# A hybrid decoder layer on one core: the second half's dense units are placed anew among the expert steps, a part of gelu is moved six steps later, and softplus is computed in another form

## What is computed

```
xn = rmsnorm(h); q,k,v,cx,cb,cc,ga,gc = split(xn @ w_in)
# 1. stick-breaking attention (16 heads of 64, causal), beside a gated short convolution of 3 taps
z = q @ k.T / 8
log_stay  = where(s < t, log_sigmoid(-z), 0)          # = -softplus(z)
log_after = reverse_cumsum(log_stay) - log_stay
w = where(s < t, exp(log_sigmoid(z) + log_after), 0);  y_attn = w @ v
y_conv = cb * conv3(cc * cx)
h += (sigmoid(ga) * (y_attn @ w_a) + sigmoid(gc) * (y_conv @ w_c)) @ w_out
# 2. cross attention over 256 memory tokens, 4 heads
h += softmax(rmsnorm(h) @ wq @ memk.T / 16) @ memv @ wo
# 3. expert mixer: 8 heads; two top-16 searches over 128 keys, then the best 16 of the 256 pairs
u = expert_u[idx]; act = gelu(u . rmsnorm(h)); h += sum(gate * act * expert_v[idx])   # 128 experts a token
out = rmsnorm(h)
```

## Time and profile before

| | us |
|---|---|
| median of 3 runs | 2285.18 |
| lowest, highest | 2284.89, 2292.32 |
| the profiled execution | 2279.03 |
| its span in the trace | 2276.9 |
| TensorE busy | 2034.0 (89%) |
| VectorE busy | 1223.6 (54%) |
| ScalarE busy | 397.9 (17%) |

### The profile page before, as it was taken

The page is one execution under the profiler, slowest core; times in us unless marked ns, Lnnn a source line. Parts: engine busy times, 40 slices in busy tenths (PEclk is TensorE's granted clock), DMA queues, the critical chain, the costliest instruction groups (busy, mean ns, idle before and its releaser), DMA issues.

```text
span 2276.9 us, 24064 instructions
## 1 busy us (share of the span) xinstructions
PE 2034.0 (89%) x9031; PEld 1305.2 (57%) x9031; DVE 1223.6 (54%) x3078; ACT 397.9 (17%) x947; POOL 904.8 (40%) x785
## 2 busy tenths in 40 slices
PE   8999999989798889998889278899999878999997
PEld 7577886746685777785748245533333445333332
DVE  0132100013975888785748999943343999553201
ACT  2222210111212233211111022200000222100001
POOL 0000000000762333553426677754444888664422
PEclk9999999999899999999899578799999788899999
DMA  7322344324997776898859888999999999999976
GB/s 236 124 93 84 126 159 149 113 90 137 384 365 251 240 238 231 314 382 295 303 203 327 310 311 309 333 372 342 342 340 344 329 336 332 332 402 375 364 254 202
DMA packets 252440, 613.48 MB, mean 269 GB/s; under 512 B 18677, under 2 KB 121125, under 8 KB 252325
## 3 DMA queue, kind: packets, MB, share of 16 engines
q0 software_dynamic: 110592, 402.70, 49.5%
q1 hardware_dynamic: 141120, 208.17, 26.5%
q10 hardware_dynamic: 612, 1.07, 0.1%
HBM read 609.77 MB, written 2.10 MB: 269 GB/s over the span
## 4 chain that ended last, share of the span: by engine, by line
PE 72%; DVE 19%; DMA 3%; ACT 2%; issue 2%; POOL 1%; DVEq 0%; POOLq 0%; SPq 0%; ACTq 0%
PE ps L514 28%; PE ps L725 20%; PE ps L526 9%; DVE u_rows L1189 7%; PE ps L688 7%; DVE hot_a L1245 2%; PE ps L551 2%; PE ps L715 2%; PE ps L563 1%; DVE hot_b L1253 1%; DVE hot_b L1248 1%; PE ps L537 1%; DMA wring<-in_peer_w_query_dram 1%; DMA v_rows<-in_peer_v_dram,idx_turned 1%; PE ps L660 1%
## 5 line engine op out<-in xcount | busy, mean ns | idle before, releaser
L476 POOL DMA_INDIRECT u_rows<-in_peer_u_dram,idx x512 | 613.6, 1198 | 1048.5 <-DVE idx L1176 562.7
L1189 DVE CUSTOM_DVE_ANT_0 u_rows<-u_rows,xn 128x1024 f32<-128x1024 f32 x512 | 618.3, 1216 | 212.3 <-DMA u_rows<-in_peer_u_dram,idx 210.5
L514 PE MATMUL ps<-xT,wring 128*128 128x256 f32 x2560 | 578.5, 386 | 10.7 <-DVE xT L977 4.9
L514 PEld LDWEIGHTS ps<-xT,wring 128*128 128x128 f32 x2560 | 492.7, 194 | 80.7 <-DVE xT L977 4.9
L725 PE MATMUL ps<-d_rows,gates 128*128 128x512 f32 x1024 | 457.1, 599 | 0.0
L725 PEld LDWEIGHTS ps<-d_rows,gates 128*128 128x128 f32 x1024 | 189.1, 190 | 268.3 <-issue 268.3
L688 PE MATMUL ps<-v_rows,diag 64*64 64x512 f32 x2048 | 290.1, 689 | 25.2 <-DMA v_rows<-in_peer_v_dram,idx_turned 25.0
L488 POOL DMA_INDIRECT v_rows<-in_peer_v_dram,idx x128 | 146.5, 1145 | 267.0 <-PE ps L688 244.5
L715 PEld LDWEIGHTS ps<-hot_b,hot_a 128*128 128x128 f32 x1024 | 151.7, 235 | 136.1 <-DVE hot_b L1253 116.7
L715 PE MATMUL ps<-hot_b,hot_a 128*128 128x64 f32 x1024 | 161.5, 324 | 75.3 <-DVE hot_b L1253 75.2
L908 ACT ACTIVATE diag<-ident,wgt 128x64 f32<-128x64 f32 x256 | 75.8, 335 | 577.3 <-PE ps L688 526.5
(11 more groups left out here) (167 smaller groups left out, 1799.9 us busy)
## 6 DMA issues: line engine op xcount, KB each, us to landing
wring<-in_w_in_dram SPq DMA_DIRECT2D x128, 512.0 KB, 5.9
d_rows<-in_peer_v_dram SPq DMA_DIRECT2D x128, 512.0 KB, 6.8
wring<-in_peer_w_query_dram SPq DMA_DIRECT2D x32, 512.0 KB, 6.6
wring<-in_w_branch_conv_dram SPq DMA_DIRECT2D x16, 512.0 KB, 6.1
wring<-in_w_branch_attn_dram SPq DMA_DIRECT2D x16, 512.0 KB, 4.6
wring<-in_w_out_dram SPq DMA_DIRECT2D x16, 512.0 KB, 4.9
wring<-in_xattn_wq_dram SPq DMA_DIRECT2D x16, 512.0 KB, 4.7
wring<-in_xattn_wo_dram SPq DMA_DIRECT2D x16, 512.0 KB, 5.6
```

What stands on the lines that cost most here:

```text
L476: pool.indirect_dma_start(out=u_rows[:, n % URING, :], out_offset=None, in_=peer_u[0], in_offset=bass.IndirectOffsetOnAxis(ap=idx[:, g % I ...
L514: mm = pe.matmul(bank(job)[:, 0:HN], w[:, k % 4, P * b:P * (b + 1)], act[:, k, :], start=(k == 0), stop=(k == KT - 1))
L1189: dve.tensor_tensor_reduce(out=u, in0=u, in1=(xn2 if h else xn1)[:, i, :], scale=1.0, scalar=0.0, op0=ALU.mult, op1=ALU.add, accum_out=dot ...
```

## The change

Three edits.

**Slots.** A unit's slot is now the step number that is reached when each kind advances by its own pace. With the two tables, the numbers worked out from the code for half 1 are:

| unit | step before | step now |
|---|---|---|
| n1 tile 0, tile 1 | 26, 26 | 26, 27 |
| first z | 58 | 55 |
| lo of head 8 | 95 | 87 |
| first gc | 133 | 118 |
| last wa | 183 | 162 |
| wo 0, wo 1 | 184, 187 | 164, 167 |
| n2 tile 0, tile 1 | 191, 192 | 171, 173 |
| first xq | 192 | 176 |
| s tile 0, tile 1 | 205, 207 | 188, 192 |
| p tile 0, tile 1 | 208, 209 | 196, 198 |
| first o | 210 | 200 |
| xo 0, xo 1 | 213, 217 | 205, 208 |
| n3 tile 0, tile 1 | 220, 221 | 212, 215 |
| pq 0, pq 8 | 222, 249 | 218, 247 |

**Gelu.** Parts 5, 6 and 7 of half 0's gelu (they need ScalarE's `gelu_exp`) move from positions 5 to 7 of the group to positions 11 to 13, for all groups but the last of half 0. ScalarE's `gelu_exp` stays at position 5.

**Softplus.** It was max(z, ln(1 + exp(min(z, 40)))); it is max(z, 0) + ln(1 + exp(-|z|)). VectorE's `min` goes, ScalarE takes |z| out of PSUM instead, and the second VectorE operation does maximum and sum in one.

```diff
     def attention_units(h):
-        units = [(kind, h, 0) for kind in ("z", "min", "exln", "max", "hi", "lo")]
+        units = [(kind, h, 0) for kind in ("z", "exln", "max", "hi", "lo")]
...
             if more:
-                units += [("z", h, hd + 1), ("min", h, hd + 1)]
+                units.append(("z", h, hd + 1))
...
-    COST = {"n1": 1, "q": 7, "k": 7, "v": 7, "z": 1, "c": 2, "y": 2, "cj": 3.5, "gc": 3.5, "ga": 3.5, "wc": 3.5,
...
-        SLOT[unit] = S_FIRST + int((S_LAST - S_FIRST) * seen / total)
+    PACE = {"n1": 1.0, "q": 2.8, "k": 2.8, "v": 2.8, "z": 0.6, "c": 0.6, "y": 0.7, "cj": 1.33, "gc": 1.44, "ga": 1.44,
...
+        SLOT[unit] = int(reached)
+        reached += PACE.get(unit[0], 0)
...
                 elif kind == "exln":
                     a = spb[:, 0:span(h)]
+                    act.wait_ge(z_done, head(h, n) + 1)
+                    if head(h, n):
+                        act.wait_ge(lo_done, head(h, n))
+                    act.activation(a, zbuf(h, n), ACT.Abs).then_inc(zc_done, 1)
                     act.wait_ge(zc_done, head(h, n) + 1)
-                    act.activation(a, a, ACT.Exp).then_inc(ez_done, 1)
+                    act.activation(a, a, ACT.Exp, scale=-1.0).then_inc(ez_done, 1)
...
-                elif kind == "min":
-                    dve.wait_ge(z_done, head(h, n) + 1)
-                    if head(h, n):
-                        dve.wait_ge(lo_done, head(h, n))
-                    dve.tensor_scalar(spb[:, 0:span(h)], zbuf(h, n), SP_CAP, None, ALU.min).then_inc(zc_done, 1)
                 elif kind == "max":
                     dve.wait_ge(lnz_done, head(h, n) + 1)
-                    dve.tensor_tensor(spb[:, 0:span(h)], spb[:, 0:span(h)], zbuf(h, n), ALU.max).then_inc(sp_done, 1)
+                    dve.scalar_tensor_tensor(out=spb[:, 0:span(h)], in0=zbuf(h, n), scalar=0.0, in1=spb[:, 0:span(h)],
+                                             op0=ALU.max, op1=ALU.add).then_inc(sp_done, 1)
...
+                late = 6 if g < HG else 0
-                if 0 < g <= GROUPS and e < 8:
+                if 0 < g <= GROUPS and e < 5:
                     gelu(g - 1, e)
+                if 0 < g <= GROUPS and 5 <= e - late < 8:
+                    gelu(g - 1, e - late)
```

More of the change, by code:

```diff
@@ L15 @@
 EPS = 1e-6
-SP_CAP = 40.0
 GELU_C = 2.0 * 0.7978845608028654
@@ L161, in group @@
         return (g // 2, g % 2, 0) if g < HG else ((g - HG) % PH, (g - HG) // PH, 1)
-    COST = {"n1": 1, "q": 7, "k": 7, "v": 7, "z": 1, "c": 2, "y": 2, "cj": 3.5, "gc": 3.5, "ga": 3.5, "wc": 3.5,
-            "wa": 3.5, "wo": 7, "n2": 2, "xq": 7, "s": 3, "p": 2, "o": 1, "xo": 7, "n3": 2, "pq": 7.5}
-    S_FIRST, S_LAST = 26, 253
-    total = sum(COST.get(unit[0], 0) for unit in FRONT[1])
+    PACE = {"n1": 1.0, "q": 2.8, "k": 2.8, "v": 2.8, "z": 0.6, "c": 0.6, "y": 0.7, "cj": 1.33, "gc": 1.44, "ga": 1.44,
+            "wc": 1.44, "wa": 1.44, "wo": 3.5, "n2": 2.5, "xq": 3.0, "s": 4.0, "p": 2.0, "o": 0.6, "xo": 3.5, "n3": 3.0,
+            "pq": 3.7}
     SLOT = {}
-    seen = 0
+    reached = 26.0
     for unit in FRONT[1]:
-        SLOT[unit] = S_FIRST + int((S_LAST - S_FIRST) * seen / total)
-        seen += COST.get(unit[0], 0)
+        SLOT[unit] = int(reached)
+        reached += PACE.get(unit[0], 0)
     with ExitStack() as ctx:
```

## The result

The changed kernel takes 2301.05 us (median of 6 runs, 2297.23 to 2305.39), the kernel before, run beside it, 2283.05 us (6 runs, 2279.08 to 2292.32): the ratio is 1.0084, with a 95% interval of 1.0067 to 1.0101. The change makes the kernel slower by 0.84%. The forecast was 2292, less than 0.5% from no change. The time lies in the range of 2274 to 2304, but outside the forecast's own range of 2284 to 2297, on the side to which 0.26 had been given.

A forecast was written before the change was run, and what follows sets the result against it. No single engine bounds the stage; what counts is when VectorE reaches steps 263 and 272. Terms: -10 us to the end of wo, +20 in the tail, -3 behind pq, sum +7: median 2292 us, own range 2284 to 2297, wide range 2274 to 2304.

The forecast's parts named there:

- Start of half 1: Half 1's first q waits for tile 1's norm, one step later than before: +1.5 us.
- Weights: In q, k, v VectorE runs freely, so its gathers make weight loads late: +4 us, between 0 and 8.
- rival 2: Weights starve at 8 us, attention gains only 4, tails cost 22: +21 us, 2306; chance 0.18.
- Attention: Half 1's attention: VectorE no longer late at lo, TensorE's clock partly recovers; -12 us, at most 15, at least 4.
- the lower bound's case: In half 1's attention, half clock returns at the 1.07 us gaps, so the gain is only 4 us.
- Softplus: ScalarE's added |z| work is covered by TensorE's products, 6 us at the least; priced at nothing elsewhere.
- Gates and wo: VectorE is ahead, so TensorE's wait before wo shrinks, -2.5 us, and idle time in the window before, -1.
- n2: From wo 1 to n2 tile 1, more and dearer VectorE steps between waiting units: +4 us.
- s and p: Cross attention, s 0 to p 1: 4 + 4 + 2 VectorE steps in place of 2 + 1 + 1; +10 us.
- n3: From xo 1 to n3 tile 1: 4 + 3 VectorE steps in place of 3 + 1; +6 us.
- From `pq` to step 272: TensorE's path still decides, barely; behind step 224 only gelu's part 5 changes, its 3.3 us wait going: -3 us.
- Behind step 272: The second half is the same program, only displaced, so nothing more changes.

The follow-up runs named there:

- gelu_only: The kernel before with only gelu's parts 5 to 7 of half 0 six steps later; 2293.01 us, ratio 1.0062.
- stops_back: The changed kernel with gelu's late parts back at positions 5 to 7 in groups 2 and 3 alone; 2296.49 us, ratio 1.0044.
- the wide rows: Changed kernel, and kernel before with only gelu moved, each loading half 1's q, k, v weights in 4 KB rows (wrong values); 2299.91 and 2290.19 us.
- tail_close: The changed kernel with half 1's serial units from n2 to pq 0 set close together; 2278.88 us, ratio 0.9999 to the kernel before.
- joined: The changed kernel with tail_close's slots, stops_back's gelu places and half 1's tile 1 norm at step 26; 2272.00 us, ratio 0.9931 to the kernel before.
- slots_only: The kernel before with the new table of paces alone, gelu and softplus as before; 2307.92 us, ratio 1.0123.
- wide_again: The changed kernel with half 1's q, k, v loads in 4 KB rows (wrong values), beside the changed kernel; 2296.16 us, 1.0068 of the kernel before.
- lead_four: The changed kernel with GpSimd running four gathers ahead in place of eight in steps 24 to 71; 2301.31 us, 1.0061 of the kernel before.

## Why the prediction was right or wrong

Measured by its own steps, from the profiles; the forecast of each stands first.

- **Start of half 1, +1.5.** It was +0.5 (`q` at 622.2 for 621.7 us).
- **Weights, +4 (0 to 8).** Mis-sized: `q` to `c` grew by 8.8, 6.4 of it waits for `wring` (above). That was rival 2's price. The mechanism held as far as it went: weights late because VectorE runs free (`gelu_only`, `stops_back`). Issues from 640 to 672 us, before and then after (count, size, median us to landing):

```profile
wring<-in_w_in_dram SPq DMA_DIRECT2D x8, 512.0 KB, 7.5
u_rows<-in_peer_u_dram,idx POOLq DMA_INDIRECT x12, 7.9
```

```profile
wring<-in_w_in_dram SPq DMA_DIRECT2D x8, 512.0 KB, 16.1
u_rows<-in_peer_u_dram,idx POOLq DMA_INDIRECT x18, 7.7
```

  The gathers land as fast as before, and the weights take twice as long. I had split the missing transfers between the two, though the earlier trace rows had shown the weights late and not the gathers (8.1 us), and I had weighed the Trainium skill's rule (DMA: Bandwidth & Descriptors, section on queues, rings and completion order) without the size of a packet. If its packets are the ones that the profile counts, the rule gives the gathers 3.6 times the bytes of the loads while both have work. The queues' rows show 8.99 to 3.49 MB, 2.6 times: the direction is the trace's, and the wide rows bear it out, but the share isn't. The Trainium skill speaks there of packets of several descriptors each, and no run here shows what one holds. What I had drawn from the rule, 0 for this term, was wrong.
- **Attention, -12 (-15 to -4).** It was -8.2. The three middle waits for `lo` went, 4.3 us for the 4.2 forecast. Of the 11 us of clock only some 4 came (what is left of the 8.2): I had left half clock only to the first and the last head. In the changed kernel it also comes in three short stretches in between, one of them here, between two heads:

```profile
786.00:789.40 3.40, 3.40 (x18) 3.40 (x19) 3.40 (x9) 3.02 (x5) 1.01 (x2) 0.54 0.20 39
```

  TensorE ran at 1.2 GHz there without an idle moment, and the only gaps ahead of it since the first head were four of 1.07 us at `wbuf`, the last of which ended 1.9 us before it:

```profile
784.13 1.78 PE L535 MATMUL ps<-qT,kT 64*128 64x256 f32 x8 [1.07 <-ACT wbuf L847]
```

  That was the lower bound's case, half clock at the gaps of 1.07 us, and it came in part; three of the thirteen gaps had such a stretch behind them, and why these three stays open. The clock in the window was 0.95 and not 0.97.
- **Softplus, 0.** In the sum it was right to give ScalarE's added operation no price; alone the edit gains 0.23%, as two of the stalls at `lo` go with the old slots.
- **Gates and wo, -3.5.** It was -3.7.
- **n2, +4.** Seen from the last sum of `wo` (it ended at 1071.5 us, 13.1 ahead of `xq`, for 9.1 before) it was +4.0; from `wo` to `xq` it is +2.3, since `wo` itself ran 1.7 us faster (27.95 for 29.64).
- **s and p, +10, and n3, +6.** They were +10.1 and +6.1. Counting the steps between two units of one chain and pricing each by its position in its group was good to a few tenths. `tail_close` confirms it: without the steps the times are gone.
- **From `pq` to step 272, -3.** This step failed, with +6.0. Three parts. The first 64 products of `pq` took 17.08 us in place of 14.05, with the clock at 1.2 GHz for longer. TensorE idled longer ahead of them, 8.7 and 6.5 us for 7.7 and 1.8, but that isn't needed for it: in `joined` the two gaps are 6.1 and 2.6 us, together less than before, and the products took 16.91. What sets the moment at which the clock returns stays open. Then weights for `pq` came late, 1.6 and 2.2 us (the timeline). And gelu's stop didn't go but grew:

```profile
1272.01 0.17 DVE L1214 TENSOR_SCALAR gl<-gl 128x16 f32<-128x16 f32 x1 [5.73 <-ACT gl L900]
```

  The forecast had that behind step 224 nothing changes but gelu's part 5. That is where it failed. ScalarE's `gelu_exp` for this stop stands at step 245, and the paces move `pq` 7 from step 246 to 244, so it now stands ahead of `gelu_exp`. ScalarE's order, before (two copies of `q` and two of the scores, `sc`, are still to come) and then after (one of `sc`):

```profile
1238.45 0.21 ACT L898 ACTIVATE gl<-gl 128x16 f32<-128x16 f32 x1
1241.42 0.38 ACT L772 ACTIVATE q<-ps 128x256 f32<-128x256 f32 x1 [2.75 <-PE ps L514]
```

```profile
1271.77 0.21 ACT L900 ACTIVATE gl<-gl 128x16 f32<-128x16 f32 x1
1272.17 0.60 ACT L888 ACTIVATE sc<-ps 128x512 f32<-128x512 f32 x1 [0.19 <-PE ps L580]
```

  One unit of `pq` takes 7.8 us (its products 6.9 and the scores' 0.9, from start to start). `slots_only`, where gelu keeps its place, has it in full: stops of 7.2 and 3.9 us, 11.1 in all, which is 3.3 and 7.8. An estimate from these numbers: the six steps by which the reader moved are 6 x 1.88 = 11.3 us, which just covers the 11.1 and leaves nothing for weights that come late. In the kernels with both edits the stop follows the late weights of `pq`: none in `tail_close` and `joined`, where no weights are late there, 2.2 us in `wide_again` (2.6 us late), 4.2 in `stops_back` (3.5), 5.7 here (3.9), 9.0 in `lead_four` (6.6). So I had moved one end of the wait and, by the slots, the other end too.
- **Behind step 272, nothing.** Of 22.0 us, 18.6 were left at the end; 3.4 came back.

So +7 was 22 at step 272, rounding aside: 9 from the stage behind `pq`, 3.8 too little for the start and the weights, 3.8 too much gained in the attention, less 1.7 at `xq`. The main mechanism, steps of VectorE between units that wait for each other, was right in place and size. Rival 2 was the nearest case, with the weights at its price, an attention that gained 8 and not 4, and tails of 18.5 and not 22. That the time lies in the stated range is owed to its width, which reached into rival 2: the forecast of +7 was less than half of what came, in the profile and in the medians.

Of the signs that had been named, the waits for `sp_lo` fell to about 7 us, those for `sp_hi` grew, and `wring` had its gap. Others weren't met: the clock of 0.97, VectorE's wait at step 224 (3.7 us, not under 3), and weights near 20 us (16.1). And one of the signs of being wrong came true: step 272 starts at 1305.5 us, 15.5 from the 1290 of the forecast, where 10 had been the limit.

## What to carry to other kernels

When units are spread evenly over an in-order engine's steps, the ones that wait for each other must still stand close together: each step between them costs its whole length as soon as no other work of the waiting engine lies beside it. An engine that is off the path and stands still for a while may be what leaves the transfers to the one that is on it; before taking its stops away, look at what it will ask for when it runs, and at the packet sizes of the transfers that will meet: here the one with the small packets lost. And a wait has two ends: before moving the reader later, look whether the same change moves other work ahead of the writer, or makes it late.

## What the runs showed of the hardware beside this

- Where gathers of 3.6 KB a packet and loads of 1.0 KB a packet met at 391 GB/s, the gathers kept their 7.7 us from issue to landing and the loads went from 7.5 to 16.1 us. With the same bytes in rows of 4 KB the loads took 8.5 us where they had taken 19.3, and the gathers 11.5 for 8.5.
- In the changed kernel's attention half clock came back in three short stretches with no longer idle time since the first head than 1.07 us. The same 64 products of `pq` took 14.05 us in some profiles and 15.5 to 17.1 us in others, also where the idle times ahead of them were together no longer (8.7 us in `joined`, 9.5 before).
